# The order inside an expert's turn, and the way into the first one, in a 32-expert encoder layer on one core

## The reference

```python
logits = (xf @ router_w) + router_b            # (256, 32)
top_v, top_i = lax.top_k(logits, 4)
gate = softmax(top_v)
# for each expert e, on the tokens that chose it:
hdn = xb @ w1[e] + b1[e]                       # 1024 -> 2048
g_, u_ = min(hdn[:, :1024], 7), clip(hdn[:, 1024:], -7, 7)
y = ((u_ + 1) * (g_ * sigmoid(1.702 * g_))) @ w2[e] + b2[e]   # 1024 -> 1024
out[token] += gate * y
x = layer_norm(alpha * x + out)
```

## Time and profile before

| | |
|---|---|
| median of 3 runs | 1196.63 us (1195.93 to 1198.13) |
| the profiled execution, its own time | 1191.44 us |
| its span, first to last instruction | 1189.6 us |
| TensorE busy | 1148.8 us, 97% |
| VectorE, ScalarE, GpSimd busy | 24%, 18%, 3% |
| granted TensorE clock, mean | 0.998 of full |
| moved by the DMA engines | 430.82 MB, 362 GB/s over the span |

### The profile page before, as it was taken

The page is one execution under the profiler, slowest core; times in us unless marked ns, Lnnn a source line. Parts: engine busy times, 40 slices in busy tenths (PEclk is TensorE's granted clock), DMA queues, the critical chain, the costliest instruction groups (busy, mean ns, idle before and its releaser), DMA issues.

```text
span 1189.6 us, 14409 instructions
## 1 busy us (share of the span) xinstructions
PE 1148.8 (97%) x5828; PEld 501.5 (42%) x5828; DVE 285.9 (24%) x742; ACT 217.5 (18%) x454; POOL 33.4 (3%) x70
## 2 busy tenths in 40 slices
PE   7999999998999999999999999999999999999997
PEld 6875887753333333333333333333333333333332
DVE  1368666662111111111111111111111111111112
ACT  1245654411111111111111111111111111111112
POOL 1000222100000000000000000000000000000000
PEclk9999999999999999999999999999999999999999
DMA  8525202599999999999999999999999999999994
GB/s 334 196 92 199 94 1 77 213 345 356 409 426 428 428 427 430 429 428 430 427 429 429 428 429 429 428 429 427 430 428 429 429 428 428 428 426 428 428 426 184
DMA packets 34610, 430.82 MB, mean 362 GB/s; under 512 B 3975, under 2 KB 4151, under 8 KB 8461
## 3 DMA queue, kind: packets, MB, share of 16 engines
q1 hardware_dynamic: 33324, 428.14, 85.9%
q0 software_dynamic: 528, 1.02, 0.3%
q10 hardware_dynamic: 720, 1.15, 0.3%
HBM read 429.23 MB, written 1.06 MB: 362 GB/s over the span
## 4 chain that ended last, share of the span: by engine, by line
PE 94%; ACT 3%; DVE 1%; issue 1%; DMA 0%; POOLq 0%; POOL 0%; SPq 0%; ACTq 0%
PE bank L1440 37%; PE bank L1453 19%; PE bank L1414 5%; PE bank L1024 5%; PE bank L1400 5%; PE bank L1034 3%; PE bank L1489 3%; PE bank L1324 2%; PE bank L1426 2%; PE bank L1408 2%; ACT pool L922 2%; PE bank L1481 1%; PE bank L1199 1%; PE bank L1214 1%; PE bank L1206 1%; PE bank L1123 1%
## 5 line engine op out<-in xcount | busy, mean ns | idle before, releaser
L1440 PE MATMUL bank<-ring,pool 128*64 128x512 f32 x1216 | 270.4, 594 | 0.0
L1440 PE MATMUL bank<-pool 128*64 128x512 f32 x832 | 185.9, 594 | 0.0
L1440 PEld LDWEIGHTS bank<-ring,pool 128*64 128x64 f32 x1216 | 85.8, 137 | 177.1 <-issue 177.1
L1453 PE MATMUL bank<-ring,pool 128*64 128x512 f32 x604 | 135.7, 596 | 0.0
L2111 DVE TENSOR_SCALAR pool<-pool 128x128 f32<-128x128 f32 x64 | 19.3, 345 | 435.0 <-PE bank L1440 435.0
L1440 PEld LDWEIGHTS bank<-pool 128*64 128x64 f32 x832 | 58.6, 137 | 121.3 <-issue 121.3
L917 ACT ACTIVATE pool<-pool 128x512 f32<-128x512 f32 x32 | 20.2, 631 | 455.9 <-DVE pool L2123 455.9
L1453 PE MATMUL bank<-pool 128*64 128x512 f32 x420 | 95.1, 596 | 0.1
L2123 DVE TENSOR_SCALAR pool<-bank 128x512 f32<-128x512 f32 x32 | 22.2, 693 | 298.5 <-PE bank L1440 298.5
L1453 PEld LDWEIGHTS bank<-ring,pool 128*64 128x64 f32 x604 | 41.9, 137 | 90.6 <-issue 90.3
L1024 PE MATMUL bank<-pool,ring 128*128 128x256 f32 x272 | 61.6, 389 | 7.0 <-DMA ring<-in_w_in_C 7.0
(11 more groups left out here) (307 smaller groups left out, 918.6 us busy)
## 6 DMA issues: line engine op xcount, KB each, us to landing
ring<-in_exp_w SPq DMA_DIRECT2D x113, 2048.0 KB, 26.6
pool<-in_exp_w SPq DMA_DIRECT2D x76, 2048.0 KB, 27.6
ring<-in_w_out SPq DMA_DIRECT2D x2, 2048.0 KB, 7.6
pool<-in_exp_w SPq DMA_DIRECT2D x3, 1024.0 KB, 9.7
ring<-in_w_in_A SPq DMA_DIRECT2D x1, 2048.0 KB, 13.4
ring<-in_w_in_B SPq DMA_DIRECT2D x1, 2048.0 KB, 7.8
ring<-in_w_in_D SPq DMA_DIRECT2D x1, 2048.0 KB, 13.4
ring<-in_w_in_H SPq DMA_DIRECT2D x1, 2048.0 KB, 7.8
```

The costliest lines, as they stand in the source:

```text
L1440: last = mm(bank[4 + g][hp, :], lhs, row(k % 2)[:, o:o + 512], start=False, stop=(k == KD - 1), skip_group_check=(k < 2))
L1453: last = mm(bank[b][SLOTS * hf:SLOTS * hf + SLOTS, :], hidden[:, k % 4, SLOTS * (k // 4):SLOTS * (k // 4) + SLOTS], w[:, 512 * hf:512 * hf ...
```

## The change

The diff below has the hunks that alter what is done. Left out are the renamed semaphores around them (the three of the last piece's parts are now shared with the first refill; that of the epsilon is merged into another), one semaphore update that nobody waited for, and the same reordering in `last_two`.

- **Pass count ahead of gates.** VectorE computes `npass_i` right after the counts, with four instructions in place of five, and before places, selection and gates. TensorE and ScalarE wait for `s_moe` at 1, which it now sets; a second update behind the gates takes over for VectorE and SP.
- **The first gather.** Between the first gather and its turning stand the first biases. The second fixed row waits for the gather and no longer for its turning.
- **First refill in two halves.** The first piece's first row of weights is free after its first half, which has a semaphore of its own (`s_w1h`). SP fills it with the first 1024 KB of piece 10, and then the rest.
- **Combining behind the second piece.** `combine` stands behind q1 instead of q0.
- **The expert's turns.** `turn_hidden` stands ahead of `gather_turn`, and ScalarE copies the turned hidden layer ahead of the turned tokens; for that copy it waits for both turnings.
- **Biases.** The up half of the next expert's bias no longer waits for the copied hidden layer; the gate half does.

```diff
@@ weight_stream @@
-            def weight_stream(it0):
+            def weight_stream(it0, half0):
-                per, rounds = 6 * GROUP, (6 * FIXED_E - NBUF) // (6 * GROUP)
+                e, q = stream[NBUF]
+                sp.wait_ge(s_w1h, half0)
+                sp.dma_start(w2b[0][:, 0:2], ew2[e][q - 4][:, 0:2]).then_inc(s_row[0], 16)
+                used(it0, 0)
+                sp.dma_start(w2b[0][:, 2:4], ew2[e][q - 4][:, 2:4]).then_inc(s_buf[0], 16)
+                first = NBUF + 1
+                per, rounds = 6 * GROUP, (6 * FIXED_E - first) // (6 * GROUP)
...
             sp.wait_ge(s_moe, 2)
-            sp.wait_ge(s_gtr2, 1)
+            sp.wait_ge(s_gath, 1)
             sp.dma_start(fixed_w1[:, 1:2], ew1[FIXED_E][0][:, 1:2]).then_inc(s_fixed, 16)
-            weight_stream(0)
+            weight_stream(0, 1)
@@ ScalarE @@
-            act.wait_ge(s_moe, 2)
+            act.wait_ge(s_moe, 1)
...
-            def hidden_turned(it, dst):
+            def hidden_turned(it, dst, read=None):
                 act.wait_ge(s_htr, it + 1)
+                if read is not None:
+                    act.wait_ge(s_gtr2, read + 1)
...
                     gate_turned(it, 6)
+                    hidden_turned(it, hT, it + 1)
                     tokens(it + 1, it)
-                    hidden_turned(it, hT)
                     expert_out(it, 6)
@@ TensorE, first_layer @@
+                        if q == 0 and n == 1 and half_used:
+                            last.then_inc(s_w1h, 1)
...
-                    if q == 0 and with_combine is not None:
+                    if q == 1 and with_combine is not None:
@@ TensorE, expert @@
-            def next_biases(it):
+            def all_biases(it):
+                pe.wait_ge(s_gtev, it + 1)
+                out_biases(it, 6)
+                bias_rows((1,))
                 pe.wait_ge(s_htev, it + 1)
-                bias_rows((0, 1)).then_inc(s_esu, 1)
+                bias_rows((0,)).then_inc(s_esu, 1)
...
                 turn_gates(it, 6)
+                turn_hidden(it)
                 gather_turn(it + 2)
-                turn_hidden(it)
-                pe.wait_ge(s_gtev, it + 1)
-                out_biases(it, 6)
-                next_biases(it)
+                all_biases(it)
@@ TensorE, before the first expert @@
-            pe.wait_ge(s_moe, 2)
+            pe.wait_ge(s_moe, 1)
...
                 gather_next(p * NE)
+                pe.wait_ge(s_esel, p * NE + 1)
+                pe.wait_ge(s_yev, p * NE + 1)
+                bias_rows((0, 1)).then_inc(s_esu, 1)
                 gather_turn(p * NE + 1)
-                pe.wait_ge(s_esel, p * NE + 1)
-                bias_rows((0, 1)).then_inc(s_esu, 1)
@@ VectorE @@
             dve.wait_ge(s_msk, NCH)
+            link(V.tensor_reduce(small[:, 12:13], bank[4][:, 0:NE], X, ALU.max))
+            link(V.tensor_scalar(small[:, 16:16 + MAXPASS], iota[:, 0:SLOTS:SLOTS // MAXPASS], float(MAXPASS),
+                                 small[:, 12:13], ALU.mult, ALU.is_lt))
+            link(V.tensor_reduce(small[:, 12:13], small[:, 16:16 + MAXPASS], X, ALU.add))
+            V.tensor_scalar(npass_i[:, :], small[:, 12:13], 0.0, None, ALU.add).then_inc(s_moe, 1)
             link(V.scalar_tensor_tensor(mcum, pview(6, 0, NCH, NE), 1.0, msk, ALU.add, ALU.mult))
...
             link(V.memset(gatex[:, :, NE * MAXPASS:], 0.0))
-            V.tensor_reduce(small[:, 12:13], bank[4][:, 0:NE], X, ALU.max).then_inc(s_moe, 1)
-            dve.wait_ge(s_moe, 1)
...
-            V.tensor_scalar(npass_i[:, :], small[:, 16:17], 1.0, None, ALU.add).then_inc(s_moe, 1)
+            nc.vector.sem_inc(s_moe, 1)
             dve.wait_ge(s_moe, 2)
```

More of the change, by code:

```diff
@@ L509, in encoder_kernel @@
         s_finp = sem("last_x2_half_ready")
-        s_eps = sem("epsilon_ready")
-        s_end = [sem(f"last_w2_rows{j}_loaded") for j in range(3)]
+        s_row = [sem(f"row_load{j}_landed") for j in range(3)]
         s_comb = sem("expert_before_last_combined")
@@ L594, in used @@
                     sp.wait_ge(s_w2, it * 2 + q - 3)
-            def weight_stream(it0):
-                per, rounds = 6 * GROUP, (6 * FIXED_E - NBUF) // (6 * GROUP)
+            def weight_stream(it0, half0):
[6 more added lines that the diff above has]
+                per, rounds = 6 * GROUP, (6 * FIXED_E - first) // (6 * GROUP)
                 with sp.Fori(0, rounds) as g:
-                    for j in range(per):
+                    for j in range(1, per + 1):
                         used(it0 + g * GROUP + j // 6, j % 6)
                         load(NBUF + j, g * GROUP + (NBUF + j) // 6, (NBUF + j) % 6)
-                for n in range(NBUF + per * rounds, len(stream)):
+                for n in range(first + per * rounds, len(stream)):
                     e, q = stream[n - NBUF]
@@ L1503, in loaded @@
                     n = nth[m, q]
+                    if n == NBUF and lead is not None:
+                        pe.wait_ge(s_row[0], lead)
                     pe.wait_ge(s_buf[n % NBUF], base + (16 * (n // NBUF) + 16))
@@ L1509, in pieces_of, with expert, last_two @@
                 return loaded
-            def expert(it, loaded):
+            def expert(it, loaded, half_used=False):
                 pe.wait_ge(s_xs, it + 1)
-                first_layer(loaded, it)
+                first_layer(loaded, it, half_used)
                 gather_next(it + 1)
                 turn_gates(it, 6)
+                turn_hidden(it)
                 gather_turn(it + 2)
-                turn_hidden(it)
-                pe.wait_ge(s_gtev, it + 1)
-                out_biases(it, 6)
-                next_biases(it)
+                all_biases(it)
                 for h in range(2):
                     second_layer_half(h, loaded, hT, 6)
-            def last_two(a, b, base, end):
+            def last_two(a, b, base, p):
                 of_a, of_b = (pieces_of(e, e, base) for e in (NE - 2, NE - 1))
@@ L1550, in last_two @@
                 for i, rows in enumerate(((0, 1), (2,), (3,))):
-                    pe.wait_ge(s_end[i], end)
+                    pe.wait_ge(s_row[i], p * 16 + 16 if i else p * 32 + 32)
                     for j in rows:
@@ L2005, in _ @@
             V.tensor_scalar(al_id, ident, ALPHA, None, ALU.mult).then_inc(s_al, 1)
-            V.memset(small[:, 20:21], LN_EPS).then_inc(s_eps, 1)
+            V.memset(small[:, 20:21], LN_EPS).then_inc(s_al, 1)
             link(V.memset(hot[0:3 * NE], 0.0))
@@ L2094, in _ @@
             link(V.memset(gatex[:, :, NE * MAXPASS:], 0.0))
-            V.tensor_reduce(small[:, 12:13], bank[4][:, 0:NE], X, ALU.max).then_inc(s_moe, 1)
-            dve.wait_ge(s_moe, 1)
-            link(V.tensor_scalar(small[:, 16:17], small[:, 12:13], float(SLOTS), None, ALU.is_gt))
-            for i in range(2, MAXPASS):
-                link(V.scalar_tensor_tensor(small[:, 16:17], small[:, 12:13], float(SLOTS * i), small[:, 16:17],
-                                            ALU.is_gt, ALU.add))
-            V.tensor_scalar(npass_i[:, :], small[:, 16:17], 1.0, None, ALU.add).then_inc(s_moe, 1)
+            nc.vector.sem_inc(s_moe, 1)
             dve.wait_ge(s_moe, 2)
```

28 lines of the change are left out of this document (13 added, 15 removed).

## The result

The changed kernel takes 1189.04 us in the median (4 runs, 1188.81 to 1189.72), the kernel before beside it 1197.33 (4 runs, 1195.93 to 1198.13): a ratio of 0.994, interval 0.9916 to 0.9963. Forecast were 1193.6 and a range from 1190.5 to 1196.5. It is faster, as forecast, but by 8.3 us where 3.0 were expected, and the range missed it. In a later comparison the same pair took 1190.78 and 1192.89, a ratio of 0.9970. The size of the gain depends on something that the forecast did not have: TensorE's granted clock, which differs between executions of one kernel.

What follows compares the result with a forecast made beforehand. The prediction took the end to follow the transfers, through the piece issued after the first expert's q4. Start 2.8 plus turn 0.2 gave 3.0 us: 1188.4 for an execution, 1193.6 with 5.2 carried over; range 1190.5 to 1196.5.

Steps and rivals of the forecast that it cites:

- What bounds the kernel: Whole kernel: TensorE and weight transfers reach the end together; the end moves with the transfers, not with faster TensorE turns.
- the issue behind the gap: Weight piece issued at 301.83 us, after first expert's q4, when transfers ran dry; forecast 3.0 us earlier, moving the end.
- last full landing: Arrival of the last 2048 KB weight piece, at 1168.02 us before; forecast to come 3 us earlier.
- The start: Before the first expert: earlier pass count lets the gather start at 269.5 for 272.31, gaining 2.8 us; other bound 1.6.
- From gather to q0: First expert's start: biases now cover the copy but another stands bare; 4.3 us before, counted unchanged, bounds 0 to 0.2.
- The refill at nothing: First weight refills: earlier issues only lengthen the pause, as the queue runs dry in the same place; counted 0.
- the turn at nothing: Expert turns: 0.23 us saved each, 7.1 over 31, hidden behind transfers except the first turn's 0.23.
- The rival of three row groups that don't run side by side: At the biases: 0.55 us more a turn, less gains, gives 1210.6; 10% chance.
- The cheaper restart: Transfers behind the gap: it closes or restarts faster, 7.8 us for 10.2, end 5.4 us earlier, 1191.2; 14% chance.
- The sum: Whole kernel: 3.0 us earlier, execution 1191.44 to 1188.4; the median's unexplained 5.2 us carried over gives 1193.6.

Runs made afterwards that it cites:

- count alone: The kernel before with only the pass count computed ahead of the gates: 1190.11 us, ratio 0.9950.
- before, slowed: The kernel before, unchanged, traced a second time: profiled execution 1196.56 us; its timed median 1194.84, ratio 0.9985.
- refill alone, slowed: The kernel before with only the first refill in two halves and the second fixed row issued at the gather: 1196.64 us, ratio 0.9999.
- the one with this refill halved: The changed kernel with the refill behind the first expert's q4 also issued in two halves: 1189.57 us, ratio 0.9942.
- after, count late: The changed kernel with the pass count back behind the gates: 1195.79 us, ratio 1.0002; profiled execution 1193.59.
- count ahead, front filled: The kernel before with the pass count ahead and one unread 512-column matmul at the last logits: 1190.59 us, ratio 0.9950.
- the run with its order alone: The kernel before with only the turn reordered (hidden layer first, biases split, ScalarE's copies swapped): 1193.53 us, ratio 0.9991.
- both with the front filled: The changed kernel with one unread matmul at TensorE's wait before the last logits: 512 columns 1189.13 us, 256 columns 1189.30.
- the four with the wait filled: Unread matmul at the last logits: changed kernel 1189.13 (512 columns), 1189.30 (256); before, pass-count wait filled too, 1192.07; before with count ahead 1190.59.

## Why the prediction was wrong

- **What bounds the kernel: right.** The end hangs on the issue behind the gap. It and the last full landing go together: 299.27 and 1165.2 (after), 299.11 and 1165.55 (count alone), 301.83 and 1168.02 (before), 306.62 and 1173.1 (before, slowed), 308.61 and 1174.9 (refill alone, slowed). Over all profiled executions but the one with this refill halved, 17, the landing comes 865.7 to 866.8 us behind the issue in 15. The two others are those with a late engine, 868.1 (after, count late) and 867.8 (count ahead, front filled).
- **The start: right.** 269.77 against 269.5, so the number was read while the matmuls ran. From gather to q0 it took 4.46 for 4.3, inside the bounds. The first q4 came at 295.44 against 295.0.
- **The refill at nothing, the turn at nothing: right as far as told apart**, the turn by the run with its order alone, whose last piece landed at 1168.10, the refill by its ratio of 0.9999. A turn is 28.07 us, for 28.24: 0.17 and not 0.23. The first refill's halves did land earlier (285.4 for 288.3), and the queue ran dry in the same place, as expected. The rival of three row groups that don't run side by side, slower, did not come.
- **The cheaper restart: a rival whose condition came and whose price did not.** The piece behind the gap took 7.9 us for 10.2 and landed 4.9 us earlier (307.1 for 312.0), for which the rival gave 5.4 us at the end; the last full piece landed only 2.8 earlier. The 16 parts of the piece behind the gap took 7.4 us in the mean in both executions, and only the last part differed, 10.2 and 7.9. At the last full piece the last parts lay alike behind the means, by 2.0 us in both. So the argument that the prediction held against this rival, that another engine may be as late by the end, came true.
- **The sum: right, for one execution against the other.** 3.0 forecast; 2.56 at the issue behind the gap, 2.8 between the last landings, 2.50 between the two profiled executions, 2.6 and 2.9 at an equal clock. That it comes so near is in part luck: a late engine moves the end of one execution by up to 2 us.
- **The step that failed** is the last sentence of the sum: "The median is 5.2 us above it, unexplained by a trace; the difference is carried over". It was a term of the kernel, and of the very place that the change touches. In the execution of 1196.56, which stands for the median of 1196.63, the clock falls behind the 2.8 us that TensorE stands idle, TensorE runs at half the clock for 10.2 us, the issue behind the gap comes 4.8 us later, the last landing 5.1, and the end 5.1. The change takes the idle away, and with it these 5 us. Without the fall, 1188.4 was forecast for an execution, and 1189.04 was measured.

The gap could have been seen as a question beforehand. The profiled execution lay 4.5 us below the fastest of the three timed runs, 1195.93, while these lay within 2.2 us of each other. A difference twice the spread points to something that the profiled execution did not have, and it should have been a rival with a price of its own: gone, if the change touches what brings it on. With the idle's 5.2 us given back in whole the sum is 1196.63 - 5.2 - 3.0 = 1188.4.

## What to carry to other kernels

Compare the profiled execution's own time and mean clock with those of the timed runs before anything is added up; when they differ by more than the runs' spread, the median holds a term that the trace lacks. The mean clock says how long the falls were and not where; only the granted clock over short stretches tells one that costs nothing from one that reaches the end. In this kernel a wait of TensorE just ahead of a stretch whose delay reaches the end cost its own length, and in part of the executions also the clock behind it: the change that took 2.8 us of idle time away gained 8.3 us in one comparison and 2.1 in another, by how often the clock of the kernel before fell. Where the wait stayed, matmuls whose product nobody reads took the second part away, and made the times more even.

## What the runs showed of the hardware

- The same program, with the same 2.8 us idle stretch, kept a mean clock of 0.997 or more in 35 of 140 executions, and had less in the others. How often differed between comparisons: of the kernel before 19 of 29 executions were in the slowest group in one, 8 of 23 in another. Why is open.
- In five profiled executions the clock fell to 0.50 for 3.4 us at 265 us, behind a wait of 0.69 us among short matmuls; in nine others with the same wait it did not. The matmuls behind the wait began at 263.99 to 264.39 us in the five and at 263.45 to 263.93 in the nine; why this goes together is open. In the four with the wait filled, by 0.5 or 1.0 us of work, it did not either.
- A fall of 3.4 us at 126 us cost nothing at the end (1188.76 with it, 1188.88 without, both with the front filled). One at 265 us went with 2 to 3 us (1191.06 to 1191.93, for 1188.94). One of 10.2 us at 273 cost 5 (1196.56 for 1191.44); with one at 265 ahead of it, it was 7 (1198.36).
- How long a transfer takes that meets a drained queue varies between executions: the 2048 KB behind the gap took 7.5 to 10.5 us, with the order of before (10.2, 10.1, 8.3, 7.9) as with the changed one (7.9, 8.4, 7.5). By the semaphore events it is the last of the 16 DMA engines that varies: in before and after the mean of the sixteen was 7.4 us in both.
- The transfers keep the delay of that issue to the end: the mean of the 16 parts of the last full piece came 863.7 to 864.6 us behind the issue at the gap in all 17 executions with that one issue, the last part 865.7 to 868.1.
